# Computing the product of p with w_ple_proj after the experts instead of beside the router

## The chip, the cores and the metric

The kernel runs on one core of a Trainium2 chip. Five engines work side by side, each with its own stream of instructions, and meet at semaphores: TensorE (PE in the profile; its weight loads are PEld), VectorE (DVE), ScalarE (ACT), GpSimd (POOL), and SyncE (SP), which here only issues DMAs. The metric is the device time of the program in microseconds, the median of three runs.

## The reference

One layer of a decoder on 512 tokens (four tiles of 128), 1024 wide, all in fp32. The parts that the change touches are the last two:

```python
        x = x + merged @ w_out[i]
        h2 = rmsnorm(x, g_ffn[i]).reshape(T, D)
        idx, wts = route(h2, w_router[i], router_bias[i])
        moe = routed_experts(h2, idx, wts, w_exp_gate[i], w_exp_up[i], w_exp_down[i]) \
            + swiglu(h2, w_sh_gate[i], w_sh_up[i], w_sh_down[i])
        x = x + moe.reshape(B, S, D)
        ple_gate = jax.nn.sigmoid(rmsnorm(x, g_ple[i]) @ w_ple_gate[i])
        x = x + ple_gate * rmsnorm(p[i] @ w_ple_proj[i], g_ple_post[i])
```

`p` is 512 x 256, `w_ple_proj` 256 x 1024 (1 MB), there are 64 experts of 1024 x 256, and eight of them are taken for each token. `p @ w_ple_proj` depends on nothing that the layer computes, and is used in the last line only.

## The kernel before

Each engine's work is written out by hand in the order in which it runs; no scheduler changes it. The order of TensorE's code is the order of its products. Semaphores carry the waits (`ple_ps`, `ple_copied`, ...). There are four stages:

- **Dense** (0 to about 430 us). Projections, attention, gates, the output projection (`out_proj`), then h2 and its transpose (`second_T`, L1241 on TensorE, copied by VectorE at L916), the transposes of `p` (L1442, copied to `pT` at L933), the router's logits (L1470), their transposes (L1475), ranks (L1532 to L1537), and the shared expert: `shared_up(f, n)` (L1489, f the half of the hidden width, n gate or up) and `shared_down(i)` (L1504). Weights are loaded by SyncE into slots of a ring, in the order of the table `DENSE`, each slot when its former user is done.
- **Routing** runs mostly on VectorE from L946 to L1025: top 8 of 64 experts for each token. Then `places(c)` (L1033) builds one-hot matrices for eight experts at a time, `lists(c)` (L1519) multiplies them on TensorE, and L1076 to L1089 turn the products into lists of rows: each of 64 experts has 96 rows, 48 steps of 128 rows in all. `shared_mult(f)` (L1041) and `base(i)` (L1048), which adds the shared expert to x, stand between the places.
- **The expert loop** (about 434 to 1130 us). For each step POOL gathers rows by an indirect DMA, TensorE transposes them, multiplies by gate and up (L1572, four experts' strips of 32 columns side by side), transposes (L1581) and multiplies by down (L1596); ScalarE weighs the result (L684) and POOL scatters it to an accumulator in HBM. SyncE loads four experts ahead, each into a slot that TensorE has left.
- **The tail**. When every scatter has landed (`experts_done`), SyncE fetches the rows of the accumulator, eight for each token, 4 MB a tile. VectorE adds them to x (`gather_sum`, L1188 to L1194: `x2_ready`), TensorE transposes the sum (`third_T`), VectorE copies that with the gain (L1199), TensorE multiplies it by w_ple_gate (L1694), ScalarE takes the sigmoid (L743) and VectorE forms the result (L1209, L1210). Between the loop and the tail each engine passes `further_rounds` (L326 to L337): five rounds for experts with over 96 rows, skipped here by a branch each.

The product with w_ple_proj is `ple_proj(i)` (L1459), four instructions of 512 columns for each tile. It stands around the logits: tile 0 before them, tile 1 behind them, tiles 2 and 3 behind their transposes. `ple_copy(i)` on ScalarE (L652, L655) squares and sums the two banks and then copies them to `pp`; POOL makes the reciprocal root (`rstd`, L464, L465); `ple_scale(i)` on VectorE (L940) multiplies `pp` by it and by the gain `gpost`.

## Time and profile before

| | |
|---|---|
| median of three runs | 1224.09 us (1221.55 to 1226.74) |
| the profiled execution | 1222.63 us |
| its span | 1220.8 us |
| TensorE busy | 1071.8 us (88%) |
| VectorE busy | 279.7 us (23%) |
| ScalarE busy | 178.0 us (15%) |
| chain that ended last, by engine | PE 71%, DMA 22%, issue 3%, DVE 1% |
| the largest groups in the chain | L1572 22%, DMA ring<-in_w_exp_up 20%, L1596 10% |
| DMA | 292.44 MB, mean 240 GB/s |

All times of one trace are microseconds from the start of the span. In a row of a timeline stand the start, the duration, the engine, the line, the operation with its operands and shape, and in brackets how long the engine was idle before it and what ended that. The duration of a row with several instructions reaches from the first start to the last end. An fp32 product shows as two records for each instruction.

### The profile page before, as it was taken

To read this page: it belongs to the slowest core of one execution; us is meant where nothing else is said; L and a number is where in the kernel's file an instruction comes from. 1 tells how busy PE (TensorE), PEld (TensorE's weight loads), DVE (VectorE), ACT (ScalarE), POOL (GpSimd) and SP (SyncE) were. 2 spreads that over 40 slices of the span, in tenths; PEclk is the share of its full clock that TensorE was granted. 3 is DMA by queue.
4 is the path that set the end of the run, shared out by engine and by line. 5 is a ranking of instruction groups with operands and counts; after the bars stand their busy time and mean duration, and the time that the engine had idled before them with its cause. 6 is when DMAs were issued, how large, how long until landed. Compare 5 with 4: busy or idle time off the path is not lost.

```text
span 1220.8 us, 16471 instructions
## 1 busy us (share of the span) xinstructions
PE 1071.8 (88%) x6715; PEld 464.9 (38%) x6715; DVE 279.7 (23%) x510; ACT 178.0 (15%) x308; POOL 193.6 (16%) x367
## 2 busy tenths in 40 slices
PE   6999999999989789798798889789779789889298
PEld 4644544444444433232232233223223223223187
DVE  3314620121239920010010000000000001000592
ACT  2003221300012001111111111111111111111020
POOL 3161000000000022211111121121121111111010
PEclk9999999999999889898898898899899889989599
DMA  9241112214030258977977887797797797788851
GB/s 333 67 151 54 69 35 96 76 69 182 35 155 1 104 222 296 415 294 295 403 308 295 361 354 288 330 388 292 292 416 281 301 416 292 316 365 304 331 247 52
DMA packets 72663, 292.44 MB, mean 240 GB/s; under 512 B 10204, under 2 KB 32240, under 8 KB 45616
## 3 DMA queue, kind: packets, MB, share of 16 engines
q1 hardware_dynamic: 57856, 255.92, 53.2%
q0 software_dynamic: 14192, 33.86, 7.1%
q10 hardware_dynamic: 576, 2.10, 0.4%
q8 instruction: 29, 0.48, 0.2%
q14 instruction: 10, 0.08, 0.0%
HBM read 279.26 MB, written 29.36 MB: 253 GB/s over the span
## 4 chain that ended last, share of the span: by engine, by line
PE 71%; DMA 22%; issue 3%; DVE 1%; SPq 1%; ACT 0%; POOL 0%; POOLq 0%; DVEq 0%
PE ps L1572 22%; DMA ring<-in_w_exp_up 20%; PE ps L1596 10%; PE ps L1320 9%; PE ps L1694 5%; PE ps L1422 5%; PE ps L1241 3%; PE ps L1304 2%; PE ps L1264 2%; PE ps L1489 2%; PE ps L1407 2%; PE ps L1405 2%; PE ps L1459 1%; DMA ring<-accumulator 1%; PE ps L1581 1%
## 5 line engine op out<-in xcount | busy, mean ns | idle before, releaser
L1572 PE MATMUL ps<-ring,gates 128*32 128x512 f32 x3072 | 373.6, 642 | 88.9 <-DMA ring<-in_w_exp_up 87.4
L1572 PEld LDWEIGHTS ps<-ring,gates 128*32 128x32 f32 x3072 | 110.0, 118 | 346.5 <-issue 344.4
L1596 PE MATMUL ps<-ring,poolbuf 128*32 128x512 f32 x1536 | 174.7, 595 | 1.7 <-ACT rows L684 0.9
L1106 DVE COPY poolbuf<-ps 128x256 f32<-128x256 f32 x48 | 20.4, 424 | 615.3 <-PE ps L1581 615.3
L1320 PE MATMUL ps<-actT,ring 128*128 128x512 f32 x256 | 112.3, 595 | 0.0
L507 POOL TENSOR_TENSOR tickets<-cst 128x1 f32<-128x1 f32 x93 | 18.5, 199 | 512.7 <-ACT rows L684 508.4
L1596 PEld LDWEIGHTS ps<-ring,poolbuf 128*32 128x32 f32 x1536 | 45.4, 109 | 93.4 <-issue 87.8
L678 ACT ACTIVATE gates<-ps 128x256 f32<-128x256 f32 x48 | 18.5, 385 | 399.8 <-PE ps L1572 399.8
L684 ACT ACTIVATE rows<-ps,qT 128x1024 f32<-128x1024 f32 x48 | 53.5, 1115 | 155.4 <-PE ps L1596 155.4
L1320 PEld LDWEIGHTS ps<-actT,ring 128*128 128x128 f32 x256 | 47.9, 190 | 59.6 <-issue 59.5
L464 POOL TENSOR_SCALAR st<-st 128x1 f32<-128x1 f32 (+1 forms) x20 | 9.4, 470 | 361.5 <-ACT rows L640 241.9
L1694 PE MATMUL ps<-ring,actT 128*128 128x256 f32 x256 | 57.9, 388 | 1.8 <-DVE actT L1199 1.8
L1422 PE MATMUL ps<-ring,gates 128*128 128x512 f32 x128 | 55.4, 593 | 2.1 <-DVE gates L896 2.1
L1241 PE MATMUL ps<-cst,actT 128*128 128x128 f32 x384 | 51.2, 277 | 3.8 <-DMA actT<-h_rows,stage 3.8
L517 POOL DMA_INDIRECT actT<-h_rows,stage x48 | 50.2, 1046 | 23.9 <-issue 23.0
L522 POOL DMA_INDIRECT accumulator<-rows,stage x48 | 48.9, 1018 | 27.1 <-issue 27.1
L1694 PEld LDWEIGHTS ps<-ring,actT 128*128 128x128 f32 x256 | 49.7, 195 | 9.1 <-DVE actT L1199 2.2
L1241 PEld LDWEIGHTS ps<-cst,actT 128*128 128x128 f32 x384 | 47.2, 191 | 5.5 <-issue 5.5
L673 ACT ACTIVATE gates<-ps 128x512 f32<-128x512 f32 x48 | 28.7, 597 | 74.8 <-PE ps L1241 74.8
L1422 PEld LDWEIGHTS ps<-ring,gates 128*128 128x128 f32 x128 | 24.2, 190 | 32.6 <-issue 29.7
L1096 DVE COPY gates<-ps 128x512 f32<-128x512 f32 x48 | 32.8, 683 | 4.3 <-PE ps L1241 4.3
L1581 PEld LDWEIGHTS ps<-cst,gates 128*128 128x128 f32 x96 | 15.1, 206 | 40.2 <-issue 40.2
(189 smaller groups left out, 801.8 us busy)
## 6 DMA issues: line engine op xcount, KB each, us to landing
ring<-in_w_exp_gate SPq DMA_DIRECT2D x64, 1024.0 KB, 12.1
ring<-in_w_exp_up SPq DMA_DIRECT2D x64, 1024.0 KB, 14.4
ring<-in_w_exp_down SPq DMA_DIRECT2D x64, 1024.0 KB, 10.8
ring<-accumulator SPq DMA_DIRECT2D x16, 1024.0 KB, 11.4
ring<-in_w_gate SPq DMA_DIRECT2D x8, 1024.0 KB, 8.9
ring<-in_w_in SPq DMA_DIRECT2D x5, 1024.0 KB, 12.9
ring<-in_w_out SPq DMA_DIRECT2D x4, 1024.0 KB, 5.0
ring<-in_w_ple_gate SPq DMA_DIRECT2D x4, 1024.0 KB, 11.1
```

The costliest lines, as they stand in the source:

```text
L517: pool.indirect_dma_start(hg[j], None, h2_dram, bass.IndirectOffsetOnAxis(ap=stage[:, 0, j, :], axis=0), bounds_check=T - 1, oob_is_err=Fa ...
L522: pool.indirect_dma_start(y_dram, bass.IndirectOffsetOnAxis(ap=stage[:, 1, j, :], axis=0), yrow[j], None, bounds_check=ACC_ROWS - 1, oob_i ...
L673: nc.scalar.activation(hgT[k][:, 4:8, :], bank(1).rearrange("p (k n) -> p k n", k=4), ACT.Copy).then_inc(hgT_hi_ready, 1)
L684: nc.scalar.activation(yrow[j], bank(6, 2), ACT.Copy, scale=slot_w[:, bass.ds(r, 1)]).then_inc(y_ready, 1)
L1096: nc.vector.tensor_copy(hgT[k][:, 0:4, :], bank(0).rearrange("p (k n) -> p k n", k=4)).then_inc(hgT_lo_ready, 1)
L1241: last = nc.tensor.transpose(bank(b0 + half)[:, k * width:(k + 1) * width], v[0:width, 4 * half + k, :], ident[0:width, 0:width])
L1320: last = mm(bank(m % 2), w[:, k, (m % 2) * P:(m % 2 + 1) * P], actT[:, k, :], start=(k == 0), stop=(k == KD - 1))
L1422: last = mm(bank(half), gates[:, k, i * P:(i + 1) * P], w[:, k], start=(k == 0), stop=(k == KD - 1))
L1572: last = mm(bank(2 + k)[part, :], hgT[k][:, q, part], pair_view(EXPERT_SLOT[js[c]])[:, q], start=(q == 0), stop=(q == KD - 1))
L1581: last = nc.tensor.transpose(bank(4)[:, q * P:(q + 1) * P], v[:, q, :], ident)
L1596: last = mm(bank(6 + half)[part, :], eactT[k][:, q, part], w[:, q, half * 512:(half + 1) * 512], start=(q == 0), stop=(q == 1))
L1694: last = mm(bank(half)[:, c * 256:(c + 1) * 256], actT[:, k, i * P:(i + 1) * P], w[:, k], start=(k == 0), stop=(k == KD - 1))
```

## The change

The loads, the product and what follows it move from the router's stretch to the end of the loop. `ple` leaves the table of dense loads; w_ple_proj is loaded as two halves behind the third expert, into a tile of `rows` and a quarter of `actT` that the loop does not use. On TensorE `ple_proj` stands between the skipped rounds and the first `third_T`. ScalarE squares each of the four pieces there and copies none of them; VectorE multiplies them by the gain out of the banks (`ple_gain`): three before the first sum of fetched rows, the fourth behind it. POOL's four reciprocal roots come behind `experts_done`. The scale by that root goes into the result, whose product gets a third operand. In the router's stretch `shared_up(0, 0)` now stands ahead of the logits' transposes and `shared_up(0, 1)` behind them. The lists' tiles move out of the way of `pT`.

```diff
--- before.py
+++ after.py
@@ -98,8 +98,8 @@
-    ["wa0", "wb0", "wa1", "wb1"] + [f"out{c}" for c in range(4)] + ["shg", "shu", "ple", "shd"]
-DENSE_SLOT = [u % 8 for u in range(17)] + [1, 2, 3, 4, 5, 6, 7, 8]
+    ["wa0", "wb0", "wa1", "wb1"] + [f"out{c}" for c in range(4)] + ["shg", "shu", "shd"]
+DENSE_SLOT = [u % 8 for u in range(17)] + [1, 2, 3, 4, 5, 6, 8]
...
+        w_ple = [rows[:, 3, :], flat_actT[:, 3 * D:4 * D]]
...
@@ -398,7 +399,9 @@
             sp.wait_ge(shared_ps, 2)
             load_expert(2, 2, None)
-            sp.wait_ge(ple_ps, NT)
+            sp.wait_ge(h2_stored, 16 * NT)
+            for j in range(2):
+                sp.dma_start(w_ple[j], t["w_ple_proj"][0][j * P:(j + 1) * P, :]).then_inc(ple_loaded, 16)
             sp.wait_ge(shdown_ps, 2 * NT)
             load_expert(3, 3, None)
...
@@ -497,10 +500,6 @@
-            for i in range(NT):
-                pool.wait_ge(ple_copied, i + 1)
-                rstd(st[:, 2, i:i + 1], D, 1, ple_rstd)
...
@@ -584,6 +583,9 @@
             nc.gpsimd.memset(tickets[:, 3:4], 0.0).then_inc(experts_done, 1)
             for i in range(NT):
+                pool.wait_ge(ple_squared, i + 1)
+                rstd(st[:, 2, i:i + 1], D, 1, ple_rstd)
+            for i in range(NT):
                 pool.wait_ge(ssq3_done, i + 1)
...
@@ -646,22 +648,11 @@
-            def ple_copy(i):
-                act.wait_ge(ple_ps, i + 1)
-                b = 2 if i % 2 == 0 else 4
-                nc.scalar.activation(pp[:, i, :], bank(b, 2), ACT.Square,
-                                     accum_out=st[:, 2, i:i + 1]).then_inc(act_step, 1)
-                act.wait_ge(act_step, i + 1)
-                nc.scalar.activation(pp[:, i, :], bank(b, 2), ACT.Copy).then_inc(ple_copied, 1)
-
-            ple_copy(0)
...
-            for i in range(1, NT):
-                ple_copy(i)
...
@@ -727,6 +718,10 @@
+            for i in range(NT):
+                act.wait_ge(ple_ps, i + 1)
+                nc.scalar.activation(pp[:, i, :], bank(2 + 2 * (i % 2), 2), ACT.Square,
+                                     accum_out=st[:, 2, i:i + 1]).then_inc(ple_squared, 1)
             act.wait_ge(experts_done, 1)
...
@@ -1050,10 +1037,8 @@
             places(1)
-            ple_scale(0)
             shared_mult(0)
             places(2)
-            ple_scale(1)
             shared_mult(1)
...
-            dve.wait_ge(ple_ps, NT)
...
@@ -1108,8 +1092,6 @@
             rows_T(0, 0)
-            ple_scale(2)
-            ple_scale(3)
             act_rows(0, 0)
...
@@ -1177,6 +1159,14 @@
+            def ple_gain(i):
+                if i == 0:
+                    dve.wait_ge(gpost_loaded, 16)
+                dve.wait_ge(ple_ps, i + 1)
+                dve.wait_ge(ple_squared, i + 1)
+                nc.vector.tensor_tensor(pp[:, i, :], bank(2 + 2 * (i % 2), 2), gpost, ALU.mult
+                                        ).then_inc(ple_copied, 1)
...
@@ -1206,13 +1196,19 @@
-                    link(nc.vector.tensor_tensor(sgate[i % 2][:, n], sgate[i % 2][:, n], pp[:, i, n], ALU.mult))
+                    if half == 0:
+                        dve.wait_ge(ple_rstd, i + 1)
+                        dve.wait_ge(ple_copied, i + 1)
+                    link(nc.vector.scalar_tensor_tensor(sgate[i % 2][:, n], sgate[i % 2][:, n], st[:, 2, i:i + 1],
+                                                        pp[:, i, n], ALU.mult, ALU.mult))
...
-            dve.wait_ge(ple_ready, NT)
             dve.wait_ge(base_ready, 2 * NT)
+            for i in range(NT - 1):
+                ple_gain(i)
             gather_sum(0, True)
+            ple_gain(NT - 1)
             gather_sum(0, False)
...
@@ -1444,24 +1440,20 @@
             second_T(3)
-            ple_proj(0)
...
@@ -1469,27 +1461,13 @@
             last.then_inc(logit_ps, 1)
-            ple_proj(1)
+            shared_up(0, 0)
             pe.wait_ge(logit_copied, 1)
...
             last.then_inc(logitT_ps, 1)
-            ple_proj(2)
-            ple_proj(3)
...
+            shared_up(0, 1)
...
@@ -1521,9 +1499,6 @@
-            shared_up(0, 0)
-            shared_up(0, 1)
...
@@ -1675,8 +1650,26 @@
+            def ple_proj(i):
+                b = 2 + 2 * (i % 2)
+                if i == 0:
+                    pe.wait_ge(pT_ready, 2)
+                    pe.wait_ge(ple_loaded, 32)
+                if i >= 2:
+                    pe.wait_ge(ple_copied, i - 1)
+                for half in range(2):
+                    for j in range(2):
+                        last = mm(bank(b + half), pT[:, j, i * P:(i + 1) * P],
+                                  w_ple[j][:, half * 512:(half + 1) * 512], start=(j == 0), stop=(j == 1))
+                last.then_inc(ple_ps, 1)
+
+            for i in range(NT):
+                ple_proj(i)
+
             def third_T(i):
                 pe.wait_ge(x2_ready, i + 1)
+                if i < 2:
+                    pe.wait_ge(ple_copied, NT - 1 + i)
```

TensorE in the dense part, from the last transposes of h2 to the ranks, before. In the names, `ps` is PSUM, `ring` a weight slot, `qT` holds pT and the scores, `gates` holds the router's weights and logits, `actT` is h2 transposed.

```order
L1241 MATMUL ps<-cst,rows 128x128 x16
L1459 MATMUL ps<-ring,qT 128x512 x4
L1470 MATMUL ps<-actT,gates 64x512 x8
L1459 MATMUL ps<-ring,qT 128x512 x4
L1475 MATMUL ps<-cst,gates 128x64 x4
L1459 MATMUL ps<-ring,qT 128x512 x8
L1489 MATMUL ps<-actT,ring 128x512 x16
L1534 MATMUL ps<-kT,triT 128x64
```

The same place in the changed kernel (L1462 are the logits, L1467 their transposes, L1453 shared_up, L1509 the first rank product):

```order
L1237 MATMUL ps<-cst,rows 128x128 x16
L1462 MATMUL ps<-actT,gates 64x512 x8
L1453 MATMUL ps<-actT,ring 128x512 x8
L1467 MATMUL ps<-cst,gates 128x64 x4
L1453 MATMUL ps<-actT,ring 128x512 x8
L1509 MATMUL ps<-kT,triT 128x64
```

Sixteen instructions of ple_proj are gone; eight of the sixteen of shared_up moved ahead of the transposes.

VectorE between the places, before (L1033 places, L940 ple_scale, L1041 shared_mult, L1048 base):

```order
L1033 TENSOR_TENSOR poolbuf<-cst,qT 128x768 x8
L940 SCALAR_TENSOR_TENSOR gates<-gates,st 128x1024
L1041 TENSOR_TENSOR gates<-gates,ps 128x512
L1033 TENSOR_TENSOR poolbuf<-cst,qT 128x768 x4
L940 SCALAR_TENSOR_TENSOR gates<-gates,st 128x1024
L1041 TENSOR_TENSOR gates<-gates,ps 128x512
L1033 TENSOR_TENSOR poolbuf<-cst,qT 128x768 x4
```

And in the changed kernel (L1020 places, L1028 shared_mult, L1035 base):

```order
L1020 TENSOR_TENSOR poolbuf<-cst,qT 128x768 x8
L1028 TENSOR_TENSOR gates<-gates,ps 128x512
L1020 TENSOR_TENSOR poolbuf<-cst,qT 128x768 x4
L1028 TENSOR_TENSOR gates<-gates,ps 128x512
L1020 TENSOR_TENSOR poolbuf<-cst,qT 128x768 x4
L1035 TENSOR_TENSOR xrow<-xrow,ps 128x512 x2
```

The two scales are gone; nothing else moved.

VectorE at the start of the tail in the changed kernel (L1167 ple_gain, L1178 to L1184 the sums of fetched rows, L1189 the copies of the transposed sum):

```order
L1167 TENSOR_TENSOR gates<-ps,gates 128x1024 x3
L1178 TENSOR_TENSOR ring<-ring 128x2048
L1167 TENSOR_TENSOR gates<-ps,gates 128x1024
L1182 TENSOR_TENSOR ring<-ring 128x2048 x2
L1183 TENSOR_TENSOR ring<-ring 128x1024
L1184 TENSOR_TENSOR xrow<-xrow,ring 128x1024
L1178 TENSOR_TENSOR ring<-ring 128x2048
L1189 TENSOR_TENSOR actT<-ps,gcol 128x4x128 x2
```

Before, the same rows stand there (L1188, L1192, L1193, L1194, L1188, L1199) without the four of ple_gain. On TensorE sixteen products of 128x512 now stand ahead of the first transposes of the tail.

## Rows read from the trace of the kernel before

**Rows 1.** Stages of the tail: stretch, length, busy by engine, PEclk, DMA share, GB/s

```profile
1129.80:1152.40 22.60, 0.01 (x2) 0.01 (x1) 9.33 (x5) 1.11 (x1) 1.28 (x3) 0.56 0.76 307
1156.17:1165.19 9.02, 9.02 (x34) 7.68 (x35) 8.61 (x5) 1.15 (x2) 0.75 (x1) 0.79 1.01 419
1165.19:1216.20 51.01, 51.01 (x248) 44.86 (x247) 29.75 (x30) 8.40 (x12) 4.60 (x6) 1.00 0.32 130
```

**Rows 2.** Timeline of VectorE, start of the tail

```profile
1142.60 2.29 DVE L1188 TENSOR_TENSOR ring<-ring 128x2048 f32<-128x2048 f32 x1 [16.80 <-DMA ring<-accumulator]
1145.04 2.29 DVE L1192 TENSOR_TENSOR ring<-ring 128x2048 f32<-128x2048 f32 x1
1147.52 2.29 DVE L1192 TENSOR_TENSOR ring<-ring 128x2048 f32<-128x2048 f32 x1 [0.19 <-DMA ring<-accumulator]
...
1152.51 2.29 DVE L1188 TENSOR_TENSOR ring<-ring 128x2048 f32<-128x2048 f32 x1 [0.17 <-DMA ring<-accumulator]
```

**Rows 3.** Timeline of VectorE, dense part

```profile
347.67 1.27 DVE L916 COPY actT<-ps 128x512 f32<-128x512 f32 x2
364.55 0.43 DVE L946 TENSOR_TENSOR gates<-qT,rbias 128x256 f32<-128x256 f32 x1 [15.60 <-ACT qT L662]
...
376.01 0.29 DVE L986 CAST kT<-qT 128x256 bf16<-128x256 f32 x1
...
388.16 7.03 DVE L1033 TENSOR_TENSOR poolbuf<-cst,qT 128x768 bf16<-128x768 f32 x8
395.10 1.27 DVE L940 SCALAR_TENSOR_TENSOR gates<-gates,st 128x1024 f32<-128x1024 f32 x1
...
401.57 0.68 DVE L1041 TENSOR_TENSOR gates<-gates,ps 128x512 f32<-128x512 f32 x1
```

**Rows 4.** Timeline of TensorE, dense part

```profile
347.81 5.25 PE L1459 MATMUL ps<-ring,qT 128*128 128x512 f32 x8 [1.25 <-DVE qT L933]
353.00 7.08 PE L1470 MATMUL ps<-actT,gates 128*64 128x512 f32 x16
360.01 3.70 PE L1459 MATMUL ps<-ring,qT 128*128 128x512 f32 x8
...
392.70 7.11 PE L1489 MATMUL ps<-actT,ring 128*128 128x512 f32 x16
...
402.39 5.26 PE L1504 MATMUL ps<-ring,gates 128*128 128x512 f32 x8 [1.12 <-DVE gates L1041]
```

**Rows 5.** Timeline of TensorE, three gate-and-up products of the loop

```profile
447.27 7.07 PE L1572 MATMUL ps<-ring,gates 128*32 128x512 f32 x64 [0.73 <-DVE gates L1096]
...
689.81 9.98 PE L1572 MATMUL ps<-ring,gates 128*32 128x512 f32 x64 [5.63 <-DMA ring<-in_w_exp_up]
...
1044.64 8.37 PE L1572 MATMUL ps<-ring,gates 128*32 128x512 f32 x64 [5.62 <-DMA ring<-in_w_exp_up]
```

**Rows 6.** One microsecond of the dense part, columns as in rows 1

```profile
410.00:411.00 1.00, 1.00 (x4) 0.47 (x3) 1.00 (x3) 0.00 (x0) 0.00 (x0) 1.00 0.00 0
```

**Rows 7.** Timeline of TensorE, the last product of the loop

```profile
1126.16 3.64 PE L1596 MATMUL ps<-ring,poolbuf 128*32 128x512 f32 x32 [0.94 <-ACT rows L684]
```

**Rows 8.** Branches of the skipped rounds: ns min/median/max, first and last start

```profile
L333 PEldq COMPARE_BRANCH  x5: 86/218/218, 1128.6 to 1131.6; - x5
...
L333 ACTq COMPARE_BRANCH  x5: 40/45/53, 1131.1 to 1132.9; - x5
```

**Rows 9.** Timeline of ScalarE, dense part: square, its sum, Silu

```profile
353.10 1.03 ACT L652 ACTIVATE gates<-ps 128x1024 f32<-128x1024 f32 x1 [10.95 <-PE ps L1459]
354.02 0.20 ACT L652 ACTIVATION_READ_ACCUMULATOR gates<-ps 128x1 f32 x1
...
399.85 0.60 ACT L667 ACTIVATE gates<-ps 128x512 f32<-128x512 f32 x1 [14.32 <-PE ps L1489]
```

**Rows 10.** Timeline of POOL, one short op in two places

```profile
366.67 0.19 POOL L464 TENSOR_SCALAR st<-st 128x1 f32<-128x1 f32 x1 [10.48 <-ACT gates L655]
...
1153.67 1.18 POOL L464 TENSOR_SCALAR st<-st 128x1 f32<-128x1 f32 x1 [18.67 <-ACT rows L734]
```

More of the change, by code:

```diff
@@ L1477, in _ @@
             last.then_inc(logitT_ps, 1)
-            ple_proj(2)
-            ple_proj(3)
-            def shared_up(f, n):
-                u = ("shg", "shu")[n]
-                if f == 0:
-                    loaded(u)
-                pe.wait_ge(ple_copied, NT - 1 + f)
-                w = unit_view(DENSE_SLOT[DENSE_AT[u]], KD)
-                for k in range(KD):
-                    last = mm(bank(2 + 2 * f + n), w[:, k, f * P:(f + 1) * P], actT[:, k, :], start=(k == 0),
-                              stop=(k == KD - 1))
-                if n == 1:
-                    last.then_inc(shared_ps, 1)
+            shared_up(0, 1)
             def shared_down(i):
```

42 lines of the change are left out of this document (16 added, 26 removed).

## The prediction

> **What bounds the kernel now.** I read the chain of waits first, then the table by stages, then each engine in order of time at the two places that the change touches. In [rows 1] the expert loop and the tail show one limit each. In the tail TensorE is busy for all of 1165.19 to 1216.20, at the full clock, and for all of 1156.17 to 1165.19, where it still starts at the half clock (mean 0.79). Whatever moves the start at 1156.17 moves the end. Before that TensorE does nothing for 22.6 us (busy 0.01): the rows of the accumulator are being fetched. What the tail waits for last is VectorE: [rows 2] shows it idle for 16.80 us until the first fetched rows are there at 1142.60, then adding until x2 of tile 0 is done at 1152.34 (the next sum starts at 1152.51, 0.17 later). One more sum of 2.29 and two copies, and TensorE is released. So from 1142.60 on each microsecond given to VectorE moves the end, and before it VectorE has 16.8 us to give.
>
> In the dense part the end is set by routing. VectorE starts it at 364.55 when the logits are transposed, hands the selection over at 376.3 and builds the places from 388.16 [rows 3]; TensorE beside it runs product behind product [rows 4]. When the lists are done, the gathers and the loop start. The loop takes up any shift: its loads are issued when TensorE frees a slot, so it begins and ends later by the same amount.
>
> **The moved product in the dense part, TensorE and ScalarE.** Before, ple_proj(0) starts at 347.81 and takes 5.25, the logits 7.01 behind it, ple_proj(1) some 3.6 more (360.01; [rows 4]), and at 364.55 VectorE has the scores. Now the logits stand directly behind the transposes and need all eight h2T pieces: the last copy ends at 347.67 + 1.27 = 348.94 [rows 3], 1.1 us later than the old product began. TensorE is at the half clock there, as before. What that costs I take from the loop: there the product of 64 records (fp32 instructions show as two records each) stands 14 times behind an idle TensorE of 5.6 to 6.8 us; it then takes between 8.37 and 9.98, mostly 9.2 to 9.8, against 7.07 without ([rows 5]: the two ends and one warm). A cold start costs 1.3 to 2.9, usually 2.4. The old ple_proj(0) paid 1.7 of it. So the logits end at 348.95 + 7.0 + 2.4 = 358.4. Behind them the new order puts shared_up(0, 0), 7.0 as at 392.70 [rows 4], ahead of the logits' transposes, which themselves wait only for a copy of 0.6. With 0.4 for the transposes and as much for the scores, VectorE starts at 366.2, against 364.55: **routing starts 1.7 us later**. The two removed ple_proj of 8.9 us did not buy anything there, because 7.0 of shared_up and a later, colder start take their place. The removed copies of ScalarE and the four small powers of POOL were off the path.
>
> **The dense part, VectorE.** Two of the four ple_scale stood on the path, 1.27 each and 1.20 from start to start at 395.10 [rows 3]: 2.4 us less. The other two ran while TensorE did the first 64-product of the loop and cost nothing before. By VectorE alone the balance is 1.7 - 2.4 = -0.7. But TensorE no longer keeps up. Its two shared_up are now done at 372.6, and the selection comes at 376.3 + 1.7 = 378.0: 5.4 us idle, which is about the length behind which the loop's rows show a cold start. shared_up(1, 0) then takes 7.0 + 2.4, to 387.9; the places of chunk 0 are there at 388.16 + 1.7 + 3.5 = 393.4, again 5.5 us idle; the lists take 0.6, and shared_up(1, 1) starts cold once more at 394.0 and ends at 403.4. ScalarE's Silu takes 0.6 ([rows 9]), so shared_mult(1) can run at 404.1. VectorE is there at 400.8 and waits 3.3 us. Before, it ran at 401.57. Everything behind it (shared_act, shared_down(0), the next places) hangs on it: **the lists come 2.5 us later**, not 0.7 earlier. The low bound is -0.7 (no cold start at either place), the high one 3.7 (2.9 for each). In shared_down(0) part may come back, if TensorE is warm there; it was not in before (5.26 for eight records at 402.39, where ple_proj warm takes 3.6). I take 2.3 for this part.
>
> **The load.** w_ple_proj is 1 MB in either kernel. It leaves the stretch at 282 and follows the third expert's 3 MB at about 404. In that window the queues are empty a little later ([rows 6]: 0 GB/s from 410 to 411), and nothing reads it for 700 us: nothing. If it did delay expert 3, 1 MB at the 425 GB/s of full DMA is 2.4 us, on a load that is issued 26 us later.
>
> **The tail.** TensorE's last product of the loop ends at 1126.16 + 3.64 = 1129.80 [rows 7], but its sequencer still has to go through the five skipped rounds, whose last branch stands at 1131.6 and takes 0.2 [rows 8]. ple_proj(0) starts at 1131.9. ScalarE leaves its own rounds at 1133.0, before the first product ends. One ple_proj is 3.5 us warm, one Square 1.03 and 0.20 for its sum [rows 9], one ple_gain about 1.27, the time of the 1024-wide scale in [rows 3] (1.20 from start to start). There are two pairs of banks, each freed by the gain. Warm: products end at 1135.4, 1138.9, 1142.4, 1145.9; squares at 1136.6, 1140.1, 1143.6, 1147.1; gains at 1137.9, 1141.4, 1144.9. The first sum of the fetched rows, which began at 1142.60, now begins at 1144.9 (+2.3) and ends at 1147.2, when square(3) is just done; ple_gain(3) adds 1.2. Then come the same sums, 1145.04 to 1152.34, less the 0.19 that VectorE waited for rows: 7.1. x2 of tile 0 is there at 1155.5: **+3.2**. Cold: before, the clock fell in this idle stretch. Its mean of 0.56 over 22.6 us ([rows 1]) is 2.7 us at the full clock and the rest at the half, so it fell at about 1132.5, less than a microsecond after the new product starts. If it falls in the new kernel too, ple_proj(0) takes about 1.7 more, as at 347.81, and all of it arrives at the first sum: +4.9. I cannot tell the two apart from the rows and take **4.1**. The low bound is 1.2: only ple_gain(3), if the three others end before 1142.6. The gate's product starts cold in both (TensorE idle for 9.7 us instead of 22.6), with 2.1 lost before and 2.4 as usual. The scale by rstd inside the result turns a two-operand product into a three-operand one. The three-operand scale of 1024 takes 1.27, the two-operand sum of 2048 takes 2.29 ([rows 2, 3]), a rate and a start that are the same for both forms within some 0.05: nothing for the one product that stands on the path. POOL's four rstd run from 1136.7 to 1148.5 and are needed after 1160.
>
> [Rows 10] show POOL's short op at 0.19 us where VectorE works on small things, and at 1.18 beside the long sum at 1152.51, which keeps its 2.29 as at 1142.60. So POOL pays there, not VectorE. A rule of the Trainium skill speaks against the change. The Trainium skill ("SBUF — State Buffer", section "SBUF: two separate sides") says that the two share a port pair as an exclusive lock, held by whichever starts first, also for a two-input VectorE op against a GpSimd read: by that rule a POOL power that starts first would stop a sum. The trace agrees with the lock, and no row has VectorE on the losing side.
>
> **Sum.** 2.3 + 4.1 = 6.4 on the profiled execution's 1222.63 (span 1220.8): 1229.0. The median of the runs is 1.5 higher, so the same shift on it gives 1230.5. I say 1229.5.
>
> **Rivals.**
> (a) *TensorE stays warm or warms soon*, and VectorE's saved 2.4 us count: dense -0.7 to +0.8, tail +3.2: 1225.1 to 1227.2. For it: the clock near the gaps differs from row to row (8.37 against 9.98). Against: all 14 products behind 5.6 us of idle or more are slow.
> (b) *The tail hides it all*, the other side: the chain of product, square and gain ends before the rows land, so that only ple_gain(3) is added; with the dense part at -0.7 the total is +0.5 or less, 1222 to 1224: not slower. It decides from the point at which the third gain ends before 1142.6, 2.3 us sooner than I find. VectorE's 16.8 idle us speak for it, the five rounds and the two pairs of banks against it.
> (c) *The clock does not rise under the logits.* Before, it rose under ple_proj(0), which is gone from there. Then all of the logits' 7 us runs at half speed, and part of shared_up: 4.6 more for the logits and up to 2.4 for shared_up, 1233.6 to 1236. Against: with them alone the clock stayed up (7.08 us for 16 records at 353.00).
> (d) *POOL stops VectorE* in the first sums, twice, for the 1.0 us that POOL loses in [rows 10]: up to 2.0, 1230.5 to 1231.5.
>
> **How the numbers follow.** Forecast 0.57 (own range 1226.8 to 1232.5), (a) 0.18, (b) 0.09, (c) 0.09, (d) 0.07. The range 1224.5 to 1234.0 leaves out (b) and nearly all of (c). No change means within 0.5%, 6.1 us around 1224.09, which is about what this measurement can tell: up to 1230.2. The forecast stands at that edge: some half of it, (d) and all of (c) are slower, the other half, (a) and most of (b) are no change. Faster by 6 us would need more than every saving here: 0.04.
>
> **What would show it.** Right: L1462 (logits) starts near 349 at a clock of 0.5; routing starts at 366; TensorE idle twice for over 5 us between 372 and 394, and the clock at 0.5 behind each; VectorE waiting for Silu before the second shared_mult; in the tail the first sum begins at 1144 to 1147 plus the shift, released by a gain and not by DMA, and the gate's product starts 3 to 5 us later than the loop's end would have it. Wrong: a first sum that still waits for DMA; a routing start at or before 364.5; TensorE at the full clock between 378 and 403.

## The result and the profile after

| | before | after |
|---|---|---|
| median of the timed runs, us | 1224.44 (6 runs, 1221.55 to 1226.74) | 1229.91 (6 runs, 1228.32 to 1233.11) |
| ratio, 95% interval | | 1.0048 (1.0029 to 1.0067) |
| profiled execution, us | 1222.63 (span 1220.8) | 1230.71 (span 1228.8) |
| mean granted TensorE clock | 0.941 | 0.941 |

The medians and ratios here and below are of executions in the chip's usual state; two timed executions of one experiment ("expert 3 early") were in a slower one and are left out. A ratio is an estimate of its own with an interval; it is not the quotient of the two medians beside it and differs from that by up to 0.1%.

A second set of six runs of the changed kernel gave 1230.22 against 1224.24, ratio 1.0051 (1.0031 to 1.0072). The forecast was 1229.5. The kernel is slower by about 0.5%, at the edge between the two outcomes that the prediction gave nearly even chances.

The two profiled spans differ by 8.0 us, which is more than the 5.5 of the medians. So I cut both traces into six pieces at events that each has, and compare the lengths. "Copies of p" is the start of VectorE's copies of the transposed p (346.48 before, 348.17 after); in both kernels the last copies of h2's transpose follow 1.19 us later. "Lists" is VectorE's first copy of the lists' products (L1076 before, L1061 after).

| stage, us | before | after | difference |
|---|---|---|---|
| start to the copies of p | 346.48 | 348.17 | +1.69 |
| copies of p to start of routing | 18.07 | 20.46 | +2.39 |
| start of routing to the lists | 59.82 | 59.23 | -0.59 |
| lists to TensorE's first work on gathered rows | 9.96 | 14.03 | +4.07 |
| expert loop | 695.47 | 690.13 | -5.34 |
| end of the loop to the end | 91.00 | 96.78 | +5.78 |

The 1.69 of the first piece is variation from run to run: a second trace of the same changed kernel has 346.48, and a third one of the kernel before has 348.73. So is most of the loop's -5.34: the second trace of the changed kernel has 694.96.

**Dense part.** First TensorE in order of time (start, us, engine, line, operation, out<-in, count, idle time before and what ended it), to be held against [rows 4]:

```profile
350.74 9.98 PE L1462 MATMUL ps<-actT,gates 128*64 128x512 f32 x16 [2.48 <-issue]
360.65 7.13 PE L1453 MATMUL ps<-actT,ring 128*128 128x512 f32 x16
...
381.13 8.51 PE L1453 MATMUL ps<-actT,ring 128*128 128x512 f32 x16
395.81 0.81 PE L1497 MATMUL ps<-kT,poolbuf 128*128 128x14 bf16 x24 [6.17 <-DVE poolbuf L1020]
396.47 9.37 PE L1453 MATMUL ps<-actT,ring 128*128 128x512 f32 x16
...
407.34 3.67 PE L1482 MATMUL ps<-ring,gates 128*128 128x512 f32 x8 [0.30 <-DVE gates L1028]
...
427.67 5.70 PE L1482 MATMUL ps<-ring,gates 128*128 128x512 f32 x8
```

The logits, warm and 7.08 before, take 9.98. The two shared_up behind idle TensorE take 8.51 and 9.37 against 7.13. But shared_down(0), 5.26 before, takes 3.67. VectorE beside it, against [rows 3]:

```profile
349.36 1.28 DVE L911 COPY actT<-ps 128x512 f32<-128x512 f32 x2
368.63 0.42 DVE L933 TENSOR_TENSOR gates<-qT,rbias 128x256 f32<-128x256 f32 x1 [17.99 <-ACT qT L655]
...
399.15 0.68 DVE L1028 TENSOR_TENSOR gates<-gates,ps 128x512 f32<-128x512 f32 x1
...
406.50 0.69 DVE L1028 TENSOR_TENSOR gates<-gates,ps 128x512 f32<-128x512 f32 x1 [3.21 <-ACT gates L658]
```

The wait of 3.21 for Silu is the one that was forecast at 3.3.

**The gather, which the prediction does not mention.** The chain of waits of the changed kernel (start, us, what) holds the fetch of the first expert's rows by POOL's indirect DMA:

```profile
432.87 8.88 DMA actT<-h_rows,stage
```

SP's queue in the changed kernel issues the next expert's load 0.53 us after that:

```profile
433.40 0.33 SPq L390 DMA_DIRECT2D ring<-in_w_exp_gate  x1
```

The same two views of the kernel before, first its chain, then SP's queue:

```profile
429.39 4.81 DMA actT<-h_rows,stage
```

```profile
430.57 0.33 SPq L389 DMA_DIRECT2D ring<-in_w_exp_gate  x1
```

There the load comes 1.18 us behind, and the rows are there in 4.81 instead of 8.88. The stretch of the gather in both, after and then before (columns as in [rows 1]; the last three are clock, DMA share and GB/s):

```profile
432.87:441.75 8.88, 0.50 (x2) 0.00 (x0) 1.22 (x2) 0.00 (x0) 3.19 (x3) 0.82 0.83 316
```

```profile
429.39:434.20 4.81, 1.10 (x3) 0.21 (x1) 1.24 (x2) 0.00 (x0) 3.19 (x3) 0.85 0.58 188
```

POOL works the same 3.19 us in both. In the changed kernel the DMA engines are busier and move more, 316 GB/s against 188, and still the rows land late: most of what moves is the load. TensorE stands for it (timeline of TensorE, after):

```profile
441.89 1.94 PE L1237 MATMUL ps<-cst,actT 128*128 128x128 f32 x8 [8.53 <-DMA actT<-h_rows,stage]
```

**Tail.** The stages, against [rows 1], then TensorE and VectorE in order of time, against [rows 2]:

```profile
1132.02:1159.47 27.45, 15.67 (x32) 6.59 (x33) 14.09 (x10) 5.58 (x9) 4.27 (x11) 0.80 0.78 316
1162.99:1173.12 10.13, 10.13 (x34) 8.46 (x35) 9.09 (x5) 1.15 (x2) 1.53 (x2) 0.70 1.00 396
1173.12:1224.00 50.88, 50.88 (x249) 44.87 (x247) 29.61 (x29) 8.40 (x12) 2.21 (x4) 1.00 0.26 107
```

```profile
1134.20 1.37 PE L1662 MATMUL ps<-rows,qT 128*128 128x512 f32 x2 [2.18 <-issue]
1135.36 1.91 PE L1662 MATMUL ps<-actT,qT 128*128 128x512 f32 x2
1137.07 1.64 PE L1662 MATMUL ps<-rows,qT 128*128 128x512 f32 x2
1138.54 1.02 PE L1662 MATMUL ps<-actT,qT 128*128 128x512 f32 x2
...
1162.99 10.13 PE L1687 MATMUL ps<-ring,actT 128*128 128x256 f32 x32 [1.55 <-DVE actT L1189]
```

```profile
1140.85 1.23 DVE L1167 TENSOR_TENSOR gates<-ps,gates 128x1024 f32<-128x1024 f32 x1 [12.84 <-ACT gates L723]
1144.25 1.23 DVE L1167 TENSOR_TENSOR gates<-ps,gates 128x1024 f32<-128x1024 f32 x1 [2.18 <-ACT gates L723]
1147.69 1.23 DVE L1167 TENSOR_TENSOR gates<-ps,gates 128x1024 f32<-128x1024 f32 x1 [2.21 <-ACT gates L723]
1148.83 2.28 DVE L1178 TENSOR_TENSOR ring<-ring 128x2048 f32<-128x2048 f32 x1
1151.15 1.23 DVE L1167 TENSOR_TENSOR gates<-ps,gates 128x1024 f32<-128x1024 f32 x1
1152.29 4.61 DVE L1182 TENSOR_TENSOR ring<-ring 128x2048 f32<-128x2048 f32 x2
...
1159.33 2.28 DVE L1178 TENSOR_TENSOR ring<-ring 128x2048 f32<-128x2048 f32 x1
```

The first ple_proj takes 1134.20 to about 1139.4, 5.2 us where a warm one is four instructions (two records each) at 0.86, 3.4: cold. The first sum does not wait for DMA any more, it stands behind three gains that wait for squares. It starts 16.8 us after the loop's last product (1148.83 - 1132.02), before 12.8 (1142.60 - 1129.80).

### The profile page after: what moved, and what is told of

The parts are those of the page before. It is cut to its first block, busy times and chain, and to the rows that moved or that the text cites. A ratio compares the mean times of both kernels' runs of the same rounds, so it can differ in the third digit from the quotient of the medians.

```text
span 1228.8 us, 16474 instructions
## 1 busy us (share of the span) xinstructions
PE 1077.5 (88%) x6715; PEld 467.3 (38%) x6715; DVE 279.8 (23%) x510; ACT 174.0 (14%) x304; POOL 189.7 (15%) x367
## 4 chain that ended last, share of the span: by engine, by line
PE 69%; DMA 21%; issue 4%; DVE 4%; SPq 1%; ACT 0%; POOL 0%; POOLq 0%; DVEq 0%
PE ps L1547 21%; DMA ring<-in_w_exp_up 20%; PE ps L1571 10%; PE ps L1316 9%; PE ps L1687 5%; PE ps L1418 5%; PE ps L1237 3%; PE ps L1300 2%; PE ps L1260 2%; PE ps L1403 2%; PE ps L1401 2%; PE ps L1453 1%; PE ps L1556 1%; PE ps L1266 1%; PE ps L1662 1%
## 5 line engine op out<-in xcount | busy, mean ns | idle before, releaser
L1316 PE MATMUL ps<-actT,ring 128*128 128x512 f32 x256 | 112.3, 595 | 0.0
L1453 PE MATMUL ps<-actT,ring 128*128 128x512 f32 x64 | 32.1, 661 | 0.0
```

Source lines behind the costliest of these rows:

```text
L1316: last = mm(bank(m % 2), w[:, k, (m % 2) * P:(m % 2 + 1) * P], actT[:, k, :], start=(k == 0), stop=(k == KD - 1))
L1453: last = mm(bank(2 + 2 * f + n), w[:, k, f * P:(f + 1) * P], actT[:, k, :], start=(k == 0), stop=(k == KD - 1))
```

## The experiments

All kernels are variants of the changed one, except where said. The stages of their traces, and beside them the sum of the differences to before in all stages but the first and the loop (in these two the engines do the same work in every kernel), and what was timed against runs of the kernel before on the same chip:

| kernel | copies of p to routing | to lists | to loop | loop | loop's end to end | sum of differences | timed difference (95%) |
|---|---|---|---|---|---|---|---|
| before | 18.07 | 59.82 | 9.96 | 695.5 | 91.00 | | |
| before, again | 18.49 | 59.96 | 9.86 | 695.8 | 90.95 | | |
| before, again 2 | 18.21 | 59.91 | 9.87 | 696.7 | 90.44 | | |
| before, load held | 18.63 | 59.94 | 9.76 | 695.4 | 91.26 | +0.7 | -1.0 (-2.7 to 0.9) |
| after | 20.46 | 59.23 | 14.03 | 690.1 | 96.78 | +11.7 | +5.9 (3.5 to 8.2) |
| after, again | 20.42 | 59.20 | 13.52 | 695.0 | 93.82 | +8.1 | +6.2 (3.8 to 8.8) |
| no tail | 20.50 | 59.26 | 13.80 | 696.5 | 91.33 | +6.0 | +3.5 (1.5 to 5.6) |
| late gain | 17.54 | 58.58 | 14.15 | 693.7 | 90.56 | +2.0 | +3.5 (1.3 to 5.8) |
| warm | 17.54 | 56.99 | 12.75 | 692.1 | 96.72 | +5.2 | +6.0 (2.8 to 9.3) |
| expert 3 early | 17.54 | 58.63 | 11.56 | 695.3 | 96.73 | +5.6 | +5.3 (3.3 to 7.2) |
| load after gather | 20.33 | 59.16 | 9.72 | 691.1 | 96.75 | +7.1 | +2.4 (-0.5 to 5.5) |
| transposes first | 14.18 | 58.99 | 14.16 | 692.6 | 94.50 | +3.0 | +1.7 (-1.3 to 4.8) |
| shared_up together | 11.22 | 58.53 | 14.30 | 695.5 | 96.86 | +2.1 | -0.4 (-3.1 to 2.2) |
| all | 11.21 | 58.49 | 9.79 | 699.4 | 91.42 | -7.9 | -10.9 (-14.8 to -7.0) |

(Timed difference: ratio less one, times 1224.) A stage is read to a few tenths in one trace. A time of the whole kernel is known to 2 us at best, because the loop alone lies between 690 and 699 us. So single terms are settled by stages, and the times say whether the sum is right. Two things differ from trace to trace of one and the same order: the logits are cold in some traces and warm in others (20.3 to 20.5 or 17.54 in the first column, down to load after gather), and so is the first ple_proj of the tail (96.7 to 96.9 or 93.8 to 94.5 at the end, where the gains stand ahead of the sums).

**No tail.** The four products, squares, roots and gains are out of the tail.

```diff
-            for i in range(NT):
-                ple_proj(i)
...
-            for i in range(NT - 1):
-                ple_gain(i)
+            dve.wait_ge(gpost_loaded, 16)
             gather_sum(0, True)
-            ple_gain(NT - 1)
             gather_sum(0, False)
```

> The changed kernel without anything of the product in the tail: no ple_proj, squares, roots or gains; the result uses gpost and an old root in their place, so the term of p is left out. The dense part is the changed one. Theory: the tail's price is the delay of the first sum on VectorE, so from the loop's last product to x2 of tile 0 it is 22.5 us as before (27.3 in the changed kernel), from the loop's last product to the end of the span 91 to 92 (96.8), and the time falls by 4.5 to 5.5 from the changed kernel's 1229.9, to about 1225. What is left over before (1224.4) is the dense part: about 2 if the loop passes its delay on, 0 if the loop absorbs it. Rival: the tail's price lies in the clock of the gate's product or in the result's third operand, then removing the product leaves 2 or more of the 5.8.

Measured: 1228.94 against 1225.22, ratio 1.0029 (1.0012 to 1.0046). VectorE's timeline of this kernel waits for the fetched rows again, like before:

```profile
1151.44 2.29 DVE L1171 TENSOR_TENSOR ring<-ring 128x2048 f32<-128x2048 f32 x1 [16.67 <-DMA ring<-accumulator]
```

What follows: with the moved work gone the tail is 91.33 again, 5.45 less than in the first trace of after. But the kernel stays slower than before by 1.5 to 5.6 us. So part of the loss isn't in the tail. I had expected 1225, and that was wrong by 4 us: the piece behind the loop fell as forecast, but the dense part and the gather stand for +5.7 in this trace and not for the 2 that I had left over.

**Late gain.** The tail keeps all products, but ScalarE copies the product out of the banks, and VectorE multiplies by the gain only ahead of each result, not ahead of the sums.

```diff
+                act.wait_ge(ple_squared, i + 1)
+                nc.scalar.activation(pp[:, i, :], bank(2 + 2 * (i % 2), 2), ACT.Copy).then_inc(ple_copied, 1)
...
-            for i in range(NT - 1):
-                ple_gain(i)
             gather_sum(0, True)
-            ple_gain(NT - 1)
...
+                    ple_gain(i - 1)
                     result(i - 1)
```

> The changed kernel, full computation, but ScalarE copies each piece out of the banks behind its square, and VectorE multiplies by the gain only ahead of each result instead of ahead of the first sums. Theory: VectorE's first sum starts when its rows land, about 12.8 us after the loop's last product, x2 of tile 0 at 22.5, and the gains fit into VectorE's free time behind tile 1 (5 us and more a tile); the last one stands ahead of the last sigmoid. Time 1225 to 1225.5, the same as without the product in the tail. Rival: the pieces that TensorE and ScalarE work on in the tail still delay it (transposes of tile 0 wait for the fourth copy), or the later gains push the sums of tiles 2 and 3: then 1227 or more.

Measured: 1227.61 against 1225.22, ratio 1.0029 (1.0011 to 1.0047). VectorE's timeline of this kernel:

```profile
1143.24 2.29 DVE L1178 TENSOR_TENSOR ring<-ring 128x2048 f32<-128x2048 f32 x1 [16.60 <-DMA ring<-accumulator]
```

What follows: the products themselves are free in this stretch. The first sum waits for its rows again, 12.60 us after the loop's last product, and the end stands 90.56 after the loop, as in before. What cost the tail its time was that VectorE's gains, which wait for the squares, stood ahead of its sums. The timed 1227.61 lies above the 1225 to 1225.5 that I had expected; its ratio is that of the kernel without a tail, and its interval overlaps that of the changed kernel. So the stage carries this reading, not the time.

**Warm.** TensorE is kept busy with products whose result nobody reads.

```diff
             shared_up(0, 1)
+            for n in range(6):
+                mm(bank(0), unit_view(DENSE_SLOT[DENSE_AT["shg"]], KD)[:, n, 0:P], actT[:, n, :], start=True, stop=True)
...
             shared_up(1, 0)
+            for n in range(8):
+                mm(bank(0), unit_view(DENSE_SLOT[DENSE_AT["shg"]], KD)[:, n, 0:P], actT[:, n, :], start=True, stop=True)
             lists(0)
```

> The changed kernel with filler products on TensorE (into a bank that nobody reads) in its two idle stretches of the routing: 6 behind shared_up(0, 1), 8 behind shared_up(1, 0). Theory: the second shared_mult waited 3.2 us because shared_up(1, 0) and (1, 1) started at the half clock (8.51 and 9.37 us instead of 7.1). With filler both take 7.1, VectorE waits under 1 us for Silu, and the lists come 2 to 3 us sooner after the start of routing (59.2 us in the changed kernel from the start of routing to the first copy of the lists, now 56.5 to 57). The time falls by that, to about 1227.5, if the loop passes it on; unchanged near 1230 if the loop absorbs it. Rival: the wait is the order of the work and not the clock: then VectorE still waits over 2 us.

Measured: 1230.78 against 1225.22, ratio 1.0049 (1.0023 to 1.0076). TensorE's timeline of this kernel, then VectorE's:

```profile
376.66 7.11 PE L1453 MATMUL ps<-actT,ring 128*128 128x512 f32 x16
383.61 7.03 PE L1519 MATMUL ps<-actT,ring 128*128 128x512 f32 x16
...
392.27 7.11 PE L1453 MATMUL ps<-actT,ring 128*128 128x512 f32 x16
```

```profile
400.05 0.69 DVE L1028 TENSOR_TENSOR gates<-gates,ps 128x512 f32<-128x512 f32 x1 [0.91 <-ACT gates L658]
```

What follows: both shared_up are back to 7.11, the wait for Silu is 0.91, and routing to lists 56.99. The logits were warm in this trace, so it is to be held against the two traces of the changed order with warm logits, late gain and expert 3 early: their waits are 2.54 and 2.58, their routing to lists 58.58 and 58.63 (3.21 and 59.23 in the first trace of after). The filler takes 1.6 off both. So the cold clock makes most of the wait; 0.91 is left to the order of the work. In the time of the whole kernel 1.6 us can't be seen.

**Expert 3 early.** Gate and up of the next expert are loaded before the shared down product is done, only the third megabyte after it.

```diff
+            load_expert(3, 3, None, (0, 1))
             sp.wait_ge(shdown_ps, 2 * NT)
-            load_expert(3, 3, None)
+            load_expert(3, 3, None, (2,))
```

> The changed kernel, but gate and up of expert 3 (2 of its 3 MB) are loaded behind w_ple_proj, some 25 us sooner, and only down waits for shared_down. Theory: the first gather took 8.9 us instead of 4.8 because the 3 MB were issued 0.5 us behind it instead of 1.2 and share the queues with it. With 1 MB left the gather lands in 4.8 or less, and the loop starts 4 us sooner after the lists. If the loop passes its start on, the time falls by 4, to 1226; if the loop absorbs it (the changed kernel's loop was 5.3 us shorter than before), it stays at 1229 to 1230. Rival for the gather: its length has nothing to do with the load, then it stays near 8.9.

Measured: 1230.15 against 1225.22, ratio 1.0043 (1.0027 to 1.0059). Its chain of waits, and its SP queue:

```profile
429.40 6.40 DMA actT<-h_rows,stage
```

```profile
429.61 0.33 SPq L392 DMA_DIRECT2D ring<-in_w_exp_down  x1
```

What follows: with 1 MB issued 0.21 us behind the gather, the rows land in 6.40. In late gain 3 MB were issued 0.19 us behind the gather, and the rows landed in 9.00, in its chain of waits and its SP queue:

```profile
427.83 9.00 DMA actT<-h_rows,stage
```

```profile
428.02 0.33 SPq L390 DMA_DIRECT2D ring<-in_w_exp_gate  x1
```

So the delay goes with how much is loaded beside the gather. My 4.8 or less was wrong: 1 MB still costs 1.6 us. The loop's 695.3 is ordinary, so the earlier landing of the 2 MB bought nothing that can be seen.

**Load after gather.** The load of expert 3 waits until the first gather has landed.

```diff
             sp.wait_ge(shdown_ps, 2 * NT)
+            sp.wait_ge(gathered[0], 16)
             load_expert(3, 3, None)
```

> The changed kernel, but the third load of the loop's start (expert 3, 3 MB) waits until the first gather has landed. In the four traces with the changed order the load was issued 0.2 to 0.9 us behind the gather and the gather took 7.6 to 9.0 us; before, it was issued 1.2 us behind it and the gather took 4.8. Theory: the load shares the queues with the gather's rows. Then the gather takes at most 4.8 here, and from the first copy of the lists to the loop's start it is 10 us or less (14.0 in the changed kernel). Rival: the gather is long by itself (the lists' place, or its descriptors), then 7.6 or more stays. For the time: if the loop passes its start on, 4 us less than the changed kernel; if its own scatter of 690 to 696 us absorbs it, no difference that three rounds can tell.

Measured: 1227.53 against 1223.90, ratio 1.0020 (0.9996 to 1.0045). Its chain of waits, and its SP queue:

```profile
432.94 4.57 DMA actT<-h_rows,stage
```

```profile
437.57 0.33 SPq L390 DMA_DIRECT2D ring<-in_w_exp_gate  x1
```

What follows: the gather takes 4.57, and lists to loop 9.72 instead of 14.03, by moving nothing but the load. That shows the cause of this stage. The timed difference is +2.4 us, where the interval reaches 0; it is less than that of the changed kernel as expected, but the two intervals overlap.

**Transposes first.** The logits' transposes stand ahead of shared_up(0, 0).

```diff
             last.then_inc(logit_ps, 1)
-            shared_up(0, 0)
...
             last.then_inc(logitT_ps, 1)
+            shared_up(0, 0)
             shared_up(0, 1)
```

> The changed kernel with the logits' transposes directly behind the logits, and both shared_up(0, n) behind the transposes. Theory: shared_up(0, 0) ahead of the transposes costs routing its own 7.0 us, so from the last pT copy to the start of routing it is 11 us where the logits run at the full clock and 13.5 where they start at the half (17.5 and 20.5 in the changed kernel, 18.1 before). The lists then take 58.5 to 59.2 from there as in the changed kernel, and the time falls by up to 7 us, to 1223. Rival: TensorE is what routing waits for later (the ranks come behind both shared_up), then the 7 us are lost again before the lists: over 62 from routing to lists.

Measured: 1226.77 against 1223.90, ratio 1.0014 (0.9989 to 1.0039). Its VectorE and its TensorE:

```profile
361.80 0.42 DVE L933 TENSOR_TENSOR gates<-qT,rbias 128x256 f32<-128x256 f32 x1 [11.71 <-ACT qT L655]
```

```profile
350.20 10.01 PE L1462 MATMUL ps<-actT,gates 128*64 128x512 f32 x16 [2.47 <-issue]
361.28 14.00 PE L1453 MATMUL ps<-actT,ring 128*128 128x512 f32 x32
```

What follows: routing starts 14.18 us after the copies instead of 20.46, with logits just as cold (10.01). These 6.3 us are the shared_up that stood ahead (7.07 from its start to the transposes' in after), less the wait for the copy of the logits. From routing to the lists it is 58.99, so nothing is lost again behind it. I had expected 13.5 for cold logits, 0.7 too little. The sum in the table is 8.7 less than in the first trace of after, but 2.3 of that is a first ple_proj that happened to be warm (end 94.50) and not this edit. The time of 1226.77 is above the 1223 that all of it would have given.

**shared_up together.** Besides, shared_up(1, 1) stands ahead of the first lists.

```diff
             shared_up(1, 0)
-            lists(0)
             shared_up(1, 1)
+            lists(0)
```

> As e6, and shared_up(1, 1) directly behind shared_up(1, 0), ahead of the lists of chunk 0. Theory: VectorE's wait of 2.5 to 3.2 us for the second Silu goes entirely, because shared_up(1, 1) is done before the places of chunk 1 are: from routing to the lists 55.5 to 56.5 us. Together with e6 some 10 us less than the changed kernel in the dense part, the time at 1220 if the loop passes it on. Rival: the lists of chunk 0 come later and hold back the places of chunk 2 (which need its buffer), then 58 or more.

Measured: 1224.28 against 1223.90, ratio 0.9997 (0.9975 to 1.0018). Its TensorE and its VectorE:

```profile
373.50 13.98 PE L1453 MATMUL ps<-actT,ring 128*128 128x512 f32 x32
...
395.23 6.35 PE L1482 MATMUL ps<-ring,gates 128*128 128x512 f32 x8
```

```profile
394.40 0.68 DVE L1028 TENSOR_TENSOR gates<-gates,ps 128x512 f32<-128x512 f32 x1
...
399.02 0.69 DVE L1035 TENSOR_TENSOR xrow<-xrow,ps 128x512 f32<-128x512 f32 x1 [0.46 <-PE ps L1482]
401.61 0.69 DVE L1035 TENSOR_TENSOR xrow<-xrow,ps 128x512 f32<-128x512 f32 x1 [1.91 <-PE ps L1482]
```

What follows: the wait for Silu is gone and both products are warm. I had expected routing to lists at 55.5 to 56.5 and a time of 1220, and both were wrong: 58.53 and 1224.28. The 58.53 is the rival's number (58 or more), but not by its cause: no wait for the lists of chunk 0 is seen ahead of the places. The idle time of TensorE has moved behind the products, and now shared_down(0) is the cold one, 6.35 against 3.67, with VectorE waiting 0.46 and 1.91 for it. The cold start that was taken away at shared_up came back at the next product behind the idle time.

**All.** Late gain, expert 3 early, load after gather (here for its last part), transposes first and shared_up together, in one kernel; its edits are those above.

> Full computation, everything together: transposes first, shared_up(1, 1) early, gate and up of expert 3 loaded 25 us sooner and its down behind the first gather, ScalarE copying the pieces of the tail and VectorE's gains late. Theory: 10 us less in the dense part, 4 at the gather, 5.7 in the tail: span 1209 to 1211 where the loop takes 693, time 1210 to 1213, faster than both kernels. Rival: the loop's length makes up for its start, then the time falls by the 5.7 of the tail alone, to 1224.

Measured: 1213.74 against 1223.90, ratio 0.9911 (0.9879 to 0.9943). Its chain of waits and its VectorE:

```profile
424.02 4.63 DMA actT<-h_rows,stage
```

```profile
1140.88 2.29 DVE L1182 TENSOR_TENSOR ring<-ring 128x2048 f32<-128x2048 f32 x1 [16.70 <-DMA ring<-accumulator]
```

What follows: the repairs add up. By stages it should be 7.9 us faster than before, and 10.9 (7.0 to 14.8) were timed. It beats both kernels. Expected were 1210 to 1213; the dense part gave 9 to 10 us less than after, as forecast, the gather 4.2 and the tail 5.4. Here ple_proj was cold again, from its second tile on, and the first sum still started 12.70 us after the loop: with late gain the cold start does not reach the first sum. Its profiled execution, 1221.39, was the slowest of its seven, with the longest loop of all traces.

**Before, again, twice.** The unchanged kernel, for how far a trace moves by itself.

> The kernel before, unchanged, once more with a profile. It tells how much of the difference between the first two traces is the change and how much differs from run to run. Theory: from pT to the start of routing 17 to 19.5 (18.1), from routing to the lists 59.8, from the lists to the loop 10.0 (its fourth shared_down runs at the half clock, so the load is issued 1.2 us behind the gather), from the loop's end to the span's end 91; only the loop's length differs, between 690 and 700. Rival: the kernel before meets its load at the first gather too in many runs (12 us and more from the lists to the loop), and the first trace was a lucky one; then the collision isn't a price of the change.

> The kernel before, unchanged, a third profile, with the same expectations as the second.

Measured: 1223.56 and 1225.74. The gather took 4.71 and 4.72, with the load 1.2 to 1.3 us behind it. The stages of before agree within 0.6 us of each other, the loop within 1.3.

**After, again.** The changed kernel, timed again with its own trace.

> The changed kernel, unchanged, once more, with five rounds. Theory: from pT to the start of routing 17.5 or 20.4, from routing to the lists 58.6 or 59.2, from the lists to the loop 13.8 to 14.2, from the loop's end to the span's end 96.8. By these stages it is 6 to 9 us slower than before; the loop's length decides what one run shows. Rival: the loop makes up for a late start, then its length is under 691.5 here as in the first trace (690.1), and the ratio stays under 1.004.

Measured: 1230.22 against 1224.24, ratio 1.0051 (1.0031 to 1.0072). TensorE in its tail:

```profile
1136.74 1.10 PE L1662 MATMUL ps<-rows,qT 128*128 128x512 f32 x2 [2.16 <-issue]
1137.67 1.02 PE L1662 MATMUL ps<-actT,qT 128*128 128x512 f32 x2
1138.53 1.02 PE L1662 MATMUL ps<-rows,qT 128*128 128x512 f32 x2
```

What follows: here the first ple_proj is warm. x2 of tile 0 stands 25.69 after the loop, 3.15 more than before; in the first trace it was cold and 4.86 more. So the end came 93.82 after the loop, where I had expected 96.8 again. The gather took 8.37, slow as in the first trace (lists to loop 13.52, just under the range), and the loop was 694.96: the rival, a loop that makes up for the late start, needed less than 691.5 and a ratio under 1.004.

**Before, load held.** The kernel before with the same wait as in "load after gather".

```diff
+            sp.wait_ge(gathered[0], 16)
             load_expert(3, 3, None)
```

> The kernel before with the load of expert 3 held until the first gather has landed, as in e5. Theory: the kernel before has little of this collision, so nothing is gained: from the lists to the loop 9.7 to 10, time within 0.2% of before. Rival: before meets the collision in a share of its runs, then the median falls by up to 4 us.

Measured: 1224.21 against 1224.24, ratio 0.9992 (0.9978 to 1.0007), gather 4.62. What follows: the kernel before has no such collision to be rid of. The 4 us belong to the changed kernel.

## Why the prediction came out

The time, the mechanism in both places and the choice between the rivals were right. Of the terms, one was missing, and what made up for it is not fully settled. So that the number fits within half a microsecond is in part luck.

- **Routing starts 1.7 us later.** 2.39 in the first trace, 2.35 in the second. The step is right in kind: the logits' cold start was 2.9 where I took 2.4. But it isn't there each time. In five of the ten traces with the logits directly behind the copies they took 7.05; in three of these five shared_up(0, 0) stood ahead of the transposes as in the changed kernel, and routing started 0.5 earlier than before. By these ten traces "usually 2.4" should have been an even chance of 0 and 3. Transposes first shows that shared_up(0, 0) ahead of them is the larger price in either case.
- **VectorE, -2.4 and a wait of 3.3; lists 2.5 later, taken as 2.3.** The wait was 3.21. From the start of routing to shared_mult(1), 37.87 after and 37.02 before: +0.85, where the prediction has +0.9. Then 1.44 came back: shared_down(0) was warm, which the prediction left open, and VectorE, which before waited 0.25 and 1.03 for it ahead of its first two base additions, waits no more. The lists came 1.8 later where I took 2.3. The warm kernel shows the cause, and its 0.91 is also what the prediction's sum has without a cold start (404.1 - 2.4 against 400.8).
- **The load costs nothing.** Right for w_ple_proj itself, as far as any trace shows. What failed is "When the lists are done, the gathers and the loop start", which takes the stretch from the lists to the loop as unchanged. The gather is issued 5.0 us behind the lists in every trace. But the last shared_down, whose end releases SP's 3 MB, took 6.31 to 6.52 in the four traces with the old order and 5.14 to 6.02 in all ten with the new one. So SP issues the load at most 0.9 us behind the gather instead of 1.2 (0.53 in the first trace), and the gather lands 3 to 4 us later. Why this shared_down is shorter, no experiment settles. I had priced a delay of the load by other transfers, never a delay of a small transfer by the load. It is the largest term of the dense part, and it is shown by holding the load, by halving what collides, and by before with the hold.
- **The tail, 4.1 (warm 3.2, cold 4.9).** x2 of tile 0 came 4.86 later cold and 3.15 later warm: both ends right, and both occur. Of the nine traces with ple_proj in the tail six have a cold one and three (after again, late gain, transposes first) a warm one. To the end of the kernel it was 5.78 and 2.82. The rest is the gate's product, which the prediction took as cold in both: 10.13 against 9.02 in the first trace, and less than before in the second.
- **Third operand, the same within 0.05.** It is 0.07: 0.75 against 0.68. For one product that stands on the path that is nothing.
- **POOL stops VectorE, rival (d).** It did not occur: the sums keep 2.28. In the changed kernel it had no chance to, since the four roots run beside the gains and between the sums; POOL pays beside the next tile's sum, in its timeline after:

```profile
1147.67 0.19 POOL L467 TENSOR_SCALAR st<-st 128x1 f32<-128x1 f32 x1 [2.60 <-ACT gates L723]
...
1160.74 0.92 POOL L467 TENSOR_SCALAR st<-st 128x1 f32<-128x1 f32 x1 [8.81 <-ACT rows L729]
```

  The case that the prediction feared, a root that starts first, is in other traces. In "all" a root's power ran on POOL from 1140.67 to 1141.22, the first sum began within it at 1140.88, and took its 2.29; in late gain the two began at 1145.67 and 1145.70, and the sum took 2.30. No sum was stopped. POOL's starts are read only roughly, but these two rows do not bear out the step "a POOL power that starts first would stop a sum".

- **Rival (a), TensorE stays warm**, occurs piece by piece: warm logits in five of ten traces, a warm ple_proj in three of nine; but shared_up(1, 1) was never warm while idle time stood ahead of it (8.70 to 9.38). **Rival (b), the tail hides all**, did not occur in any trace of the changed kernel; late gain shows that one reordering makes it true. **Rival (c)** did not occur: the logits took 9.98 and not the 14 that it needs, and shared_up behind them ran at the full clock (7.13).

My sum was 6.4 and the measured difference 5.5 and 6.0. By stages the two traces give 11.7 and 8.1: up to the lists 1.8 and 1.7 (forecast 2.3), at the gather 4.1 and 3.6 (no term), behind the loop 5.8 and 2.8 (forecast 4.1). In the table the sum of stages lies above the timed interval in three kernels (after, no tail, load after gather), and all three have cold logits in their trace. The other timed runs have no trace. If the logits are warm in some of them, that takes off up to 3 us there, and a warm ple_proj as much; this is argued and not shown. Whether the loop also gives back a little of a late start stays open: behind late starts it was 690.1 and 691.1, but also 695.0 and 696.5. So the forecast's number was helped by a missing term of +4 and by terms that don't occur in each run. It does not bear out each size.

## What to carry to other kernels

Work that moves into a stretch where its engines are idle can still cost time there. Find the engine whose work ends the stretch, here VectorE with its sums, and let nothing of the moved work stand ahead of it: the products could move for nothing, the gains could not. When a step ahead of a DMA changes its time by half a microsecond, look which two transfers now start together, and what a small gather loses to a large load. Take the half clock as a chance at each product that stands behind idle TensorE, and when you remove the idle time at one product, look at which product it stands next.

## What was not expected of the hardware

- A gather of rows by POOL's indirect DMA lands in 4.57 to 4.81 us when SP's load is issued 1.2 us or more behind it, or only when it has landed (six traces). It takes longer the closer the 3 MB load follows (seven traces): 7.60 at 0.86 us, 8.37 to 8.88 at 0.52 and 0.53, 9.00 and 9.01 at 0.19 and 0.40, 9.15 when both are issued together. With 1 MB at 0.21 us it is 6.40.
- The same product behind the same 2.5 us of idle TensorE ran at 7.05 in five traces and at 9.85 to 10.02 in the five others. In the slow ones the granted clock fell from 1.00 to 0.50 within that idle time and rose again under the product, in the fast ones it stayed at 1.00. I found nothing ahead of it in the traces that tells which of the two will occur.
- What the half clock costs where idle time ends lies between 1.4 and 2.9 us: 9.98 for 7.05 (the logits), 8.51 and 9.37 for 7.13 (shared_up), 6.35 for 3.67 (shared_down), 5.2 for 3.4 (ple_proj).
